# A decoder trunk in float32: in the later groups of the second stage, the keys' projection, taps, sigmoid and product are placed one slot sooner, and nine projection matmuls move to the first slots of an iteration

## The reference

```python
proj = rmsnorm(h) @ w_in                       # q, k, v, z for 8 heads of 128, and the gates' logits
qkv = silu(causal_depthwise_conv(proj[qkv], conv_w))          # 4 taps
q = l2norm(q) * DK ** -0.5; k = l2norm(k); z = proj[z]
# per head, in chunks of tokens (gcum: cumulated log decay, gam: decay between two tokens)
tmat = eye + strict(beta * (k @ k.T) * gam)
u, w = triangular_solve(tmat, [v * beta, k * beta * exp(gcum)])
v_new = u - w @ state                          # chunk after chunk
o = (q * exp(gcum)) @ state + ((q @ k.T) * gam) @ v_new
state = state * d_last + k_dec.T @ v_new
out = (rmsnorm(o) * silu(z)) @ w_out
```

## Time and profile before

| what | value |
| --- | --- |
| median of three runs | 2801.99 us (2800.05 to 2802.21) |
| the profiled execution, its own time | 2798.55 us |
| its span | 2796.6 us |
| TensorE matmuls (PE) busy | 2498.3 us, 89% of the span |
| weight loads (PEld) busy | 2193.1 us, 78% |
| VectorE busy | 1671.3 us, 60% |
| ScalarE busy | 1132.8 us, 41% |
| GpSimd busy | 481.3 us, 17% |
| iterations 8 to 31 of the second stage | from 550.8 to 1542.6 us of the span |

### The profile page before, as it was taken

One profiled execution on the slowest core, in us unless ns is written; L12 is line 12 of the kernel. 1 busy time (PEld: TensorE's weight loads), 2 busy tenths in 40 slices (PEclk: granted clock), 3 DMA queues, 4 the chain that ended last, 5 costly groups with the idle time before them and its releaser, 6 DMA issues. The chain is left out here.

```text
span 2796.6 us, 50391 instructions
## 1 busy us (share of the span) xinstructions
PE 2498.3 (89%) x17193; PEld 2193.1 (78%) x17193; DVE 1671.3 (60%) x3872; ACT 1132.8 (41%) x3326; POOL 481.3 (17%) x377
## 2 busy tenths in 40 slices
PE   5568887899999999999999699999996999999997
PEld 4467777789998999999999468878885777777775
DVE  4367676777777777777777333333332666666664
ACT  4244454544444444444444244433331333333332
POOL 0144343310000000000000012100001333223331
PEclk9689999999999999999999689999997999999998
DMA  6664354544445444344453167743455222222221
GB/s 194 200 245 143 137 167 147 180 132 130 143 138 189 137 145 131 126 156 134 122 164 97 27 196 257 243 158 139 182 199 229 68 68 84 84 68 75 68 69 47
DMA packets 273813, 392.78 MB, mean 140 GB/s; under 512 B 79282, under 2 KB 187906, under 8 KB 273442
## 3 DMA queue, kind: packets, MB, share of 16 engines
q1 hardware_dynamic: 240066, 370.05, 39.6%
q10 hardware_dynamic: 33632, 21.26, 2.6%
HBM read 267.92 MB, written 123.31 MB: 140 GB/s over the span
## 5 line engine op out<-in xcount | busy, mean ns | idle before, releaser
L1227 PE MATMUL p_psp<-xg,p_whi 128*128 128x264 f32 x4096 | 842.4, 295 | 26.6 <-POOL p_wlo L1176 17.2
L1227 PEld LDWEIGHTS p_psp<-xg,p_whi 128*128 128x128 f32 x4096 | 655.5, 191 | 31.2 <-issue 21.9
L1227 PE MATMUL p_psp<-xg,p_wlo 128*128 128x264 f32 x2048 | 606.9, 296 | 0.0
L1227 PEld LDWEIGHTS p_psp<-xg,p_wlo 128*128 128x128 f32 x2048 | 391.6, 191 | 0.0
L981 DVE SCALAR_TENSOR_TENSOR p_acc<-p_proj,p_taps,p_acc 128x528 f32<-128x528 f32 x288 | 251.8, 874 | 5.4
L1822 PE MATMUL first_q<-first_w,p_o 128*128 128x512 f32 (+1 forms) x864 | 208.3, 401 | 17.0 <-DVE first_w L1786 17.0
L2364 PE MATMUL first_q<-first_w,p_hT 128*128 128x512 f32 x720 | 196.4, 413 | 13.4 <-DVE p_q L2250 13.0
L1822 PEld LDWEIGHTS first_q<-first_w,p_o 128*128 128x128 f32 (+1 forms) x864 | 157.4, 184 | 61.2 <-issue 17.0
L2364 PE MATMUL p_pso<-p_wo,p_oT 128*128 128x512 f32 x768 | 194.3, 404 | 7.9 <-DVE p_oT L2276 4.2
L862 ACT ACTIVATE p_sig<-p_sig 128x528 f32<-128x528 f32 x128 | 82.5, 645 | 293.1 <-DVE p_sig L983 293.1
L2364 PEld LDWEIGHTS p_pso<-p_wo,p_oT 128*128 128x128 f32 x768 | 143.7, 192 | 48.5 <-issue 16.1
(11 more groups left out here) (265 smaller groups left out, 4664.5 us busy)
## 6 DMA issues: line engine op xcount, KB each, us to landing
p_whi<-w_dram SPq DMA_DIRECT2D x92, 512.0 KB, 4.1
p_wlo<-w_dram SPq DMA_DIRECT2D x92, 512.0 KB, 5.2
raw<-w_a_in SPq DMA_DIRECT2D x36, 512.0 KB, 6.8
w_dram<-p_whi SPq DMA_DIRECT2D x34, 512.0 KB, 4.0
w_dram<-p_wlo SPq DMA_DIRECT2D x34, 512.0 KB, 5.3
p_o<-hT_dram SPq DMA_DIRECT2D x34, 512.0 KB, 4.7
hT_dram<-p_hT SPq DMA_DIRECT2D x32, 512.0 KB, 3.3
p_hT<-hT_dram SPq DMA_DIRECT2D x30, 512.0 KB, 4.0
```

The costliest lines, as they stand in the source:

```text
L1227: ins = nc.tensor.matmul(ps_p[half_][:, 0:HALF], (w_hi, w_lo)[i][:, f, kc * P:(kc + 1) * P], xg[:, g % 2, j, kc, half_ * HALF:(half_ + 1) ...
```

## The change

For iterations 8 to 31 (`later`) other tables are used. `FILL_LATER` gives the slots 0, 1 and 2 two, three and four matmuls more, slot 4 one less, and the slots 19 to 23 two, two, two, one and one less. Units are therefore complete sooner, and `EVACUATE_LATER` evacuates unit 0 in slot 3 (before 4), unit 1 in 5 (6), unit 2 in 9 (10) and unit 3 in 11 (12); units 4 to 7 stay where they were. `SOONER` puts the work on f = 0 one slot sooner: its taps 0 and 1 from slot 7 to 6, taps 2 and 3 from 8 to 7, the fifth part from 9 to 8, the exp from 9 to 8, ln and exp from 10 to 9, and the product from 11 to 10.

```diff
+        FILL_LATER = (10, 12, 10, 8, 8, 8, 4, 10, 8, 8, 10, 8, 8, 4, 2, 5, 4, 4, 8, 11, 11, 11, 8, 12)
+        EVACUATE_LATER = {3: (0, 0), 5: (0, 1), 9: (0, 2), 11: (0, 3), 18: (0, 4), 20: (0, 5), 22: (0, 6), 0: (1, 7)}
+        SOONER = {7: 6, 8: 7, 9: 8, 10: 9, 11: 10}
...
-            base = [Slot(FILL[s] if p else 0) for s in range(len(FILL))]
+            later = bool(p) and not p[0].meta
+            base = [Slot((FILL_LATER if later else FILL)[s] if p else 0) for s in range(len(FILL))]
...
             for s, (back, f, parts) in TAPS.items():
+                s = SOONER[s] if later and f == 0 else s
                 base[s].taps += [(it - back, f, n) for n in parts if item[back]]
             for s, (back, f, parts) in SIGMOID.items():
+                s = SOONER[s] if later and f == 0 else s
                 base[s].sigmoid += [(it - back, f, n) for n in parts if item[back]]
             for s, (back, f) in SILU.items():
+                s = SOONER[s] if later and f == 0 else s
                 base[s].silu += [(item[back], it - back, f)] if item[back] else []
-            for s, (back, u) in (EVACUATE_META if opening else EVACUATE).items():
+            for s, (back, u) in (EVACUATE_META if opening else EVACUATE_LATER if later else EVACUATE).items():
                 base[s].evacuated += [(it - back, u)] if item[back] else []
```

## The result

The changed kernel is slower by 0.18%: the ratio of its time to that of before is 1.0018, with a 95% interval of 1.001 to 1.0026 (medians of 20 runs each 2807.04 and 2800.78 us; these two alone would give 1.0022). The forecast was -1.4 us, with a change of under 0.2% as the likeliest, an own range of 2795 to 2806 us and a wide one, which took in the rivals, of 2789 to 2812. The median lies in the wide one only, and the sign is wrong. The profiled execution of the changed kernel took 2796.65 us (span 2794.7), which is the shortest of its 20. So this profile shows the mechanism well, and the size badly.

The account below looks back on a forecast made before the run. The prediction took a loop through VectorE, ScalarE and the inverse as the bound: -0.50 + 0.40 us an iteration over 24, plus 1.0 us for one late load, gives -1.4 us, 2800.6 us; own range 2795 to 2806, wide 2789 to 2812.

Parts of the forecast that it names:

- the rivals: Alternative outcomes: gain stays, 2790 us, chance 0.31; slower by the inverse, 2814, 0.24; iteration's end not faster, 2812, within slower.
- What bounds: A loop through VectorE, ScalarE and the inverse sets the iteration; filling TensorE's waits pays only if that loop shortens.
- The end of the iteration, -0.50: From R (last `right`) to the queries' first tap: unit 5 complete sooner, so its evacuation follows the exp, 0.50 us less.
- The inverse, +0.40: Two taps ahead of row 15 delay the solved copy 1.36 us; beyond 1.00 us slack, `left` starts 0.40 us later.
- The row of 3.4 us for the load: Median time from issue to landing of the inverse's load in the trace, used to place the landing before `left`.
- the estimate of 2.6 us: The skill page's time for the inverse's 0.26 MB load; it would have made the sum -3.6 us; rejected for the trace.
- ks of chunk 3, +1.04 less 0.69 for the keys: New 1.04 us wait at slot 9, keys' 0.69 us wait gone: TensorE reaches `left` 0.35 us later, under the load's 0.40.
- The sum: -0.50 + 0.40 = -0.10 us an iteration, times 24 is -2.4; 1.0 more for one late load gives -1.4 us.
- The one iteration that was charged: One iteration in 23 whose `left` already waits 0.7 us for the load; without slack to give, it loses 1.0 us more.
- slower, by the inverse: Rival: loads taking 4.0 us make `left` 1.0 us later, +12 us in all, 2814 us; chance 0.24.
- The signs that the prediction set for itself: Waits about 1 us in slot 9 and at the load, solved copy 8.5 us after the state, windows 41.3 and 40.75 us.

Follow-up runs that it names:

- e6: The changed kernel with the old fills and evacuations; only the keys' taps, sigmoid and product a slot sooner: ratio to before 1.0037.
- e9: The changed kernel with the keys' taps 2 and 3 back in slot 8, taps 0 and 1 still in slot 6: ratio to before 1.0013.
- e5: The changed kernel with the new fills and evacuations alone; keys' taps, sigmoid and product in their old slots: ratio to before 0.9944.
- e8: The changed kernel with iteration 8 on the old tables, the other 23 later iterations on the new: ratio to before 1.0021.
- e4: The changed kernel with the keys' taps left in slots 7 and 8; fifth part, sigmoid and product a slot sooner: ratio to before 0.9956.
- e12: e7 unaltered, run again beside e11 on the same chip for a second profile: ratio to before 0.9908.
- e3: The changed kernel with row 15 and the solved copy done ahead of the keys' taps in slot 6: ratio to before 0.9962.
- e7: The changed kernel with the keys' taps in their old slots and the sigmoid spread over slots 8, 9 and 10, product in 11: ratio to before 0.9916.
- e11: e7 with iteration 8 on the old tables: ratio to before 0.9926.
- e10: e7 with the loads of the next group's input issued after the inverse's stores and loads instead of ahead: ratio to before 0.9982.

## Why the prediction was wrong

*What bounds.* Right. The loop through VectorE and the inverse sets the time, not TensorE's waits: e6 removes one wait of 12.1 us in all and is slower by 0.37%, and e9 removes one of about 15 us, has 12.2 us of it back at another place and 5 us less wait for the load, and gains nothing.

*The end of the iteration, -0.50.* Right, -0.61. The evacuation even starts 0.10 us ahead of the exp's end. The fills alone (e5) are worth -0.6%.

*The inverse, +0.40.* Right: the solved copy 1.37 us later, `left` 0.35. The slack of 1.00 us is that of a typical iteration; in iteration 21 itself, whose load took 4.0 us, it was 0.44. The row of 3.4 us for the load held, not the estimate of 2.6 us from the Trainium skill, page "DMA: Bandwidth & Descriptors", section "Anatomy of one DMA — SWDGE (gpsimd) path": the shortest load is again 3.2 us.

*ks of chunk 3, +1.04 less 0.69 for the keys.* The new wait is there with 0.93 us on that path, and free, as was said, since the load ends the wait at `left`.

*The sum.* This is the step that failed. It took a typical iteration 24 times, charged 1.0 us more for one iteration whose load is late, and put iteration 8 and the granted clock at nothing. What a typical iteration is was right to 0.08 us. Three things stand against the rest.

First, late loads. With the slack of 1.00 us spent, each late load lengthens its iteration, not one of them. In the two profiles the iterations 9 to 30 should take 901.6 and 901.1 us by their own medians; they take 905.7 and 904.0, so 4.1 and 2.9 us more, of which up to 1.7 are the half clock of iteration 10. In the two of before the same difference is -0.7 and +0.5. That is +3.6 us, or 2.8 without that clock, where I had +1.0, and it eats the gain of 22 x -0.16 = -3.5: these 22 iterations take on average what they took before (904.3 and 905.4 us). It varies: with the inverse as late, e8 has 3.1 and e9 1.4, and with slack left e4, e5 and e12 have 0.8 to 1.3, but e3 and e7 4.1 and 4.0, nearly all of it in an iteration 16 with half clock. So the sign of this term is clear at `left`, and its size is not well known. The one iteration that was charged, 16, got no longer (42.4 and 42.0 us, before 42.4 and 43.3); the longer ones are others. The rival "slower, by the inverse" names this ("carry each scatter to the end"), but prices it as if all loads were late.

Second, iteration 8. It was priced as typical; it was 2.8 us longer in the mean, with the pause of 2.84 us and the stretches at half clock. Together the later iterations take 994.8 and 995.3 us against 991.8 and 992.7, +2.8 us, which is what iteration 8 alone makes.

Third, what the profiles do not show. The profiled executions themselves differ by -1.9 and +1.1 us, the medians of the executions by +4.5. Take off each median's difference to before what its typical iteration makes in 24: the changed kernel, e8 and e9 are left with +7 to +9 us, and e3, e4, e5, e7 and e12, which have slack left, with -0.5 to +2.7. That speaks for the late inverse. But e6, which has it too, has only 2.9 (5 executions), and e11, which has not, 4.5 (5 executions).

e3 shows that the late inverse is the cause of the loss: with the solved copy ahead of the taps the kernel is 0.38% faster than before, not 0.1 to 0.2% slower. The signs that the prediction set for itself (the waits, the copy, the window) came nearly all as said, and so did the typical iteration: none of them could tell that the sum was wrong.

*What stays open.* By which way the late inverse costs some 6 us beyond the typical iteration (15 against 8.4 us in e3), and whether the granted clock is lower because of the change. It is by 0.0015 in the mean, some 2.4 us, of which the stretch behind the pause of iteration 8 would be 1.7 if every execution has it. Late loads make pauses of over 1 us, and the clock fell after the one of iteration 10, but not after the longer one of iteration 17 in the second profile. But before against itself had 0.9550 in one session, and e6, which has the late loads too, 0.9562. No run here separates a late load from its clock.

## What to carry to other kernels

Removing a wait pays only as far as the loop that sets the period gets shorter. So follow the release of each wait back until the chain closes on itself, and price the change along that loop, with every engine's order within a slot. Ahead of a two-way trip through memory, keep slack between landing and use: once it is spent, every late landing goes into the time, and a sum of typical iterations does not hold it. Price the first iteration of a loop by its own rows, since its waits can be others. And a profile can be the best of twenty: for a difference of a few tenths of a per cent, take the size from many executions and only the mechanism from the trace.

## What the runs showed of the hardware

In iteration 8 a pause of TensorE of 2.7 to 2.8 us came with 3.4 us at a granted clock of 0.50, in four profiles of four. After the pause of 1.36 us in iteration 10 the granted clock was 0.54 for 3.4 us; other pauses as long had no such stretch behind them (1.36 us in iteration 16 of the same profile, 1.6 us in iteration 17 of the second), so the one is not shown to cause the other. An issue on SyncE can itself take long: in e10 that of one weights' load took 7.72 us right behind the group's input, and 5.32 us in iteration 8, against a median of 0.36 us, and everything behind it in that queue was late. Why it took so long, no run here shows.
